# Prompt attention of a hybrid encoder step: value products with the values as weights, both heads of a pair in one output bank

## The reference

```
s = einsum('bqhc,bkc->bhqk', q_lat, ckv) + einsum('bqhr,bkr->bhqk', q_pe, kpe)
s = s.astype(jnp.float32) * MLA_SCALE
mask = (k_pos[None, :] // CHUNK) <= (q_pos[:, None] // CHUNK)      # CHUNK = 64
s = jnp.where(mask[None, None], s, jnp.finfo(jnp.float32).min)
p = jax.nn.softmax(s, axis=-1).astype(ckv.dtype)
o_lat = jnp.einsum('bhqk,bkc->bqhc', p, ckv)
mla_out = jnp.einsum('bthc,chv->bthv', o_lat, lw['w_uv']).reshape(B, T, MLA_HEADS * MLA_V)
```

## Time and profile before

| what | value |
|---|---|
| median of 3 runs | 2654.84 us (2651.89 to 2655.52) |
| profiled execution, its own time | 2655.19 us |
| its span | 2653.4 us |
| TensorE busy, share of the span | 2588.1 us, 98% |
| VectorE busy | 1689.6 us, 64% |
| ScalarE busy | 1134.7 us, 43% |
| GpSimd busy | 437.4 us, 16% |

### The profile page before, as it was taken

How to read it: one execution, slowest core, us unless ns; L and a number is a source line. 1 busy time by engine, 2 the same in 40 slices (tenths; PEclk the granted TensorE clock), 3 DMA queues, 4 the chain that set the end, 5 groups by cost and what they waited for, 6 DMA issues and landing times. The chain is left out here.

```text
span 2653.4 us, 44721 instructions
## 1 busy us (share of the span) xinstructions
PE 2588.1 (98%) x17819; PEld 2478.6 (93%) x17819; DVE 1689.6 (64%) x2725; ACT 1134.7 (43%) x1919; POOL 437.4 (16%) x366
## 2 busy tenths in 40 slices
PE   8999999999899999999999999999989999999999
PEld 8999999996679999999999999999966799999998
DVE  5666575637666776657577575764575758657473
ACT  5343344415544434334454342553164445434253
POOL 0010112102135101011210110121122341011011
PEclk9999999999999999999999999999999999999999
DMA  3322324320015132222313223234101141332231
GB/s 111 92 80 80 95 70 106 75 55 11 24 39 94 49 91 80 80 84 75 111 33 96 80 70 90 78 81 103 30 8 34 39 97 56 91 92 70 80 87 58
DMA packets 369747, 190.74 MB, mean 72 GB/s; under 512 B 38493, under 2 KB 365488, under 8 KB 369582
## 3 DMA queue, kind: packets, MB, share of 16 engines
q1 hardware_dynamic: 365582, 178.03, 24.9%
q0 software_dynamic: 4000, 10.47, 1.7%
HBM read 182.53 MB, written 5.93 MB: 71 GB/s over the span
## 5 line engine op out<-in xcount | busy, mean ns | idle before, releaser
L716 PE MATMUL ps<-xh,w 128*128 128x320 f32 x1920 | 595.1, 310 | 3.1 <-DVE css L2891 3.1
L717 PE MATMUL ps<-xl,w 128*128 128x320 f32 x1920 | 593.3, 309 | 0.0
L718 PE MATMUL ps<-xh,w 128*128 128x320 f32 x1920 | 593.3, 309 | 0.0
L1502 ACT ACTIVATE w<-raw 128x512 fp32r<-128x512 f32 (+3 forms) x372 | 316.0, 861 | 486.9 <-PE ps L718 466.1
L716 PE MATMUL ps<-hh,w 128*128 128x320 f32 x1408 | 438.0, 311 | 3.3 <-DVE ub L2295 1.2
L718 PE MATMUL ps<-hh,w 128*128 128x320 f32 x1408 | 435.1, 309 | 0.0
L717 PE MATMUL ps<-hl,w 128*128 128x320 f32 x1408 | 435.0, 309 | 0.0
L2988 POOL TENSOR_TENSOR hl<-ub,hh 128x640 fp32r<-128x640 f32 x88 | 174.5, 1983 | 1448.1 <-ACT hh L1502 1385.3
L716 PEld LDWEIGHTS ps<-xh,w 128*128 128x128 f32 x1920 | 360.4, 188 | 5.3 <-DVE css L2891 3.6
L717 PEld LDWEIGHTS ps<-xl,w 128*128 128x128 f32 x1920 | 360.4, 188 | 0.3
L718 PEld LDWEIGHTS ps<-xh,w 128*128 128x128 f32 x1920 | 360.4, 188 | 0.0
(11 more groups left out here) (408 smaller groups left out, 4663.6 us busy)
## 6 DMA issues: line engine op xcount, KB each, us to landing
raw<-in_w_ffn_in_dram SPq DMA_DIRECT2D x176, 512.0 KB
raw<-in_w_ffn_out_dram SPq DMA_DIRECT2D x192, 192.0 KB
raw<-in_w_in_dram SPq DMA_DIRECT2D x38, 512.0 KB
raw<-in_w_ffn_out_dram SPq DMA_DIRECT2D x64, 128.0 KB
wraw<-in_w_out_dram SPq DMA_DIRECT2D x8, 512.0 KB
raw<-in_w_out_dram SPq DMA_DIRECT2D x8, 512.0 KB
out_dram<-xio SPq DMA_DIRECT2D x5, 512.0 KB
xin<-in_x_prompt_dram SPq DMA_DIRECT2D x1, 2048.0 KB, 8.2
```

Of the source, the lines that this page charges most:

```text
L716: pe.matmul(out, wh, xh, start=first, stop=False, skip_group_check=loose)
L717: pe.matmul(out, wh, xl, start=False, stop=False, skip_group_check=loose)
L718: return pe.matmul(out, wl, xh, start=False, stop=last, skip_group_check=loose)
L1502: return nc.scalar.activation(out, in_, func, **kw)
```

## The change

- The value product is turned. The values (64 columns of one head, all 128 keys of a block) are the weights, and the transposed probabilities are the moving operand. The result has value columns on the partitions and 128 queries along the free dimension. The two heads of a pair go to rows 0 to 63 and 64 to 127 of bank 6, alternately. It is done for both heads at the steps of the odd head; an even head has no value product of its own.
- The even head's transposed probabilities must last until then. They go to `PTA`, ten blocks of 128 in the second half of the tile `at`; the odd head uses `ptb` as before (`weights_of`).
- The division moves. The exponents' row sums go to a new tile `sums`. Per pair VectorE takes the reciprocals (`inverse_sums`), TensorE multiplies each of them, broadcast to 64 weight columns, with the identity (`pair_rows`: 8 matmuls of 128 columns to bank 7), ScalarE copies that to `y`, and VectorE multiplies bank 6 by it into `y` (`pair_output`). The transposes of the pair's output are gone.
- TensorE's values of a pair wait for the product of the pair before (`o_sb`). The waits of values, maxima and `head_latents` on `normalise` and on the old pair output are gone, and ScalarE's copies and exponents have other ones.
- The streams' rotated latent queries go to the end of bank 1 and no longer to bank 2; `head_queries` of the second half waits for their copy.
- The first zeroing of `at` covers its first half only. The second half is zeroed after the last values, ahead of `pnew`.
- Two dummy products after the loop, not three. The last `pair_rows` stands ahead of them. The wait for the last pair's output moves ahead of the first `level_step`.
- VectorE's wait for two stores at n = 18 moves to ScalarE's copy for pair 2.

```
+    SUMS = tile(s_w, "sums", [P, 2, PT_, 2])
+    RS = tile(s_w, "rs", [P, PT_, 2])
+    AT_HALF = TILES * 2
+    ATB = AT[:, :, :, :, :].rearrange("p t e g q -> p (t e g) q")
+    PTA = ATB[:, AT_HALF:2 * AT_HALF, :]
+    def weights_of(h, i):
+        return PTB[:, i % 2, :] if h % 2 else PTA[:, i * (i + 1) // 2:(i + 1) * (i + 2) // 2, :].rearrange("p k q -> p (k q)")
...
@@ TensorE
             if h:
                 pe.wait_ge(*q_ready.nth(l, 2 * (h - 1) + half))
                 pe.wait_ge(*qk_sb.nth(l, 2 * (h - 1) + half))
+                if half:
+                    pe.wait_ge(*ql_sb.nth(l, h - 1))
...
-            if h % 2 and h > 2:
-                pe.wait_ge(*o_sb.nth(l, h // 2 - 1))
...
         def attend_values(l, n):
             h, i = divmod(n, PT_)
             pe.wait_ge(*pt_sb.nth(l, n))
-            if n >= 2:
-                pe.wait_ge(*on_sb.nth(l, n - 2))
+            if i == 0 and h > 1:
+                pe.wait_ge(*o_sb.nth(l, h // 2 - 1))
             for k in range(i + 1):
-                mm = pe.matmul(PS[:, 6 + n % 2, 0:P], PTB[:, n % 2, k * P:(k + 1) * P],
-                               VM[:, k, h // 2 * P:(h // 2 + 1) * P], start=k == 0, stop=k == i)
+                for e in range(2):
+                    mm = pe.matmul(PS[64 * e:64 * e + 64, 6, i * P:(i + 1) * P],
+                                   VM[:, k, (h - 1 + e) * 64:(h + e) * 64], weights_of(h - 1 + e, i)[:, k * P:(k + 1) * P],
+                                   start=k == 0, stop=k == i, skip_group_check=True)
             mm.then_inc(pv_ps.sem, 1)
-        def pair_output(l, pair):
-            pe.wait_ge(*on_sb.nth(l, 8 * pair + 7))
-            pe.wait_ge(*ql_sb.nth(l, min(2 * pair + 2, H - 1)))
-            for t in range(PT_):
-                mm = pe.transpose(PS[:, 2, t * P:(t + 1) * P], Y[:, pair, t * P:(t + 1) * P], IDENT[:, :])
-            mm.then_inc(ot_ps.sem, 1)
+        def pair_rows(l, pair):
+            pe.wait_ge(*rs_sb.nth(l, pair))
+            if pair:
+                pe.wait_ge(*o_sb.nth(l, pair - 1))
+            for i in range(PT_):
+                for e in range(2):
+                    mm = pe.matmul(PS[64 * e:64 * e + 64, 7, i * P:(i + 1) * P], RS[:, i, e:e + 1].broadcast_to([P, 64]),
+                                   IDENT[:, :], start=True, stop=True)
+            mm.then_inc(rb_ps.sem, 1)
...
                 if n % 8 == 2 and n > 8:
-                    pair_output(l, n // 8 - 1)
+                    pair_rows(l, n // 8 - 1)
...
-                attend_values(l, n)
+                if h % 2:
+                    attend_values(l, n)
+            pair_rows(l, H // 2 - 1)
             pe.wait_ge(*exp_sb.nth(l, NT - 1))
             held(pe)
-            spin(PS[:, 4, :], 3)
-            pair_output(l, H // 2 - 1)
+            spin(PS[:, 4, :], 2)
...
             stream_scores(l, 0)
+            pe.wait_ge(*o_sb.nth(l, H // 2 - 1))
             level_step(l, 0)
...
@@ ScalarE
+                if i == 0 and h > 3 and h % 2 == 0:
+                    act.wait_ge(*rs_sb.nth(l, h // 2 - 2))
                 run(PB[:, n % 2, 0:(i + 1) * P], PS[:, 3 + n % 2, 0:(i + 1) * P], ACT.Exp,
-                    bias=MX[:, n % 4, 1:2], accum_out=MX[:, n % 4, 2:3]).then_inc(exp_sb.sem, 1)
+                    bias=MX[:, n % 4, 1:2], accum_out=SUMS[:, h // 2 % 2, i, h % 2:h % 2 + 1]).then_inc(exp_sb.sem, 1)
...
-                if n >= 2:
-                    act.wait_ge(*pv_ps.nth(l, n - 2))
-                run(PTB[:, n % 2, 0:(i + 1) * P], PS[:, 5, 0:(i + 1) * P], ACT.Copy).then_inc(pt_sb.sem, 1)
-            def pair_output(pair):
-                act.wait_ge(*ot_ps.nth(l, pair))
-                run(Y[:, pair, 0:TP], PS[:, 2, :], ACT.Copy).then_inc(o_sb.sem, 1)
+                before = PT_ * (h // 2) + i - (2 if h % 2 and i >= 2 else 2 if h % 2 else PT_)
+                if before >= 0:
+                    act.wait_ge(*pv_ps.nth(l, before))
+                run(weights_of(h, i)[:, 0:(i + 1) * P], PS[:, 5, 0:(i + 1) * P], ACT.Copy).then_inc(pt_sb.sem, 1)
+            def pair_rows(pair):
+                act.wait_ge(*rb_ps.nth(l, pair))
+                if pair == 2:
+                    act.wait_ge(cn_stored, 32 * (l + 1))
+                run(Y[:, pair, 0:TP], PS[:, 7, :], ACT.Copy).then_inc(rb_sb.sem, 1)
...
@@ VectorE
-            def normalise(n):
-                h, i = divmod(n, PT_)
-                dve.wait_ge(*pv_ps.nth(l, n))
-                chain.link(V.reciprocal(MX[:, n % 4, 3:4], MX[:, n % 4, 2:3]))
-                at = i * P + 64 * (h % 2)
-                out = PS[:, 6 + n % 2, 64 * (h % 2):64 * (h % 2) + 64]
-                V.tensor_scalar(Y[:, h // 2, at:at + 64], out, MX[:, n % 4, 3:4], None, ALU.mult).then_inc(on_sb.sem, 1)
+            def inverse_sums(pair):
+                dve.wait_ge(*exp_sb.nth(l, 8 * pair + 7))
+                V.reciprocal(RS[:, :, :], SUMS[:, pair % 2, :, :]).then_inc(rs_sb.sem, 1)
+            def pair_output(pair):
+                dve.wait_ge(*pv_ps.nth(l, PT_ * pair + PT_ - 1))
+                dve.wait_ge(*rb_sb.nth(l, pair))
+                V.tensor_tensor(Y[:, pair, 0:TP], PS[:, 6, :], Y[:, pair, 0:TP], ALU.mult).then_inc(o_sb.sem, 1)
...
-                if n >= 3:
-                    normalise(n - 3)
+                if n % 8 == 1 and n > 8:
+                    inverse_sums(n // 8 - 1)
+                if n % 8 == 4 and n > 8:
+                    pair_output(n // 8 - 1)
...
@@ GpSimd
-            G.memset(AT[:, :, :, :, :], 0.0).then_inc(ml_zero.sem, 1)
+            G.memset(ATB[:, 0:AT_HALF, :], 0.0).then_inc(ml_zero.sem, 1)
...
-            pool.wait_ge(*pv_ps.nth(l, NT - 1))
+            pool.wait_ge(*pv_ps.nth(l, NT // 2 - 1))
             pool.wait_ge(*pn_zero.nth(l, 1))
             held(pool)
+            G.memset(ATB[:, AT_HALF:2 * AT_HALF, :], 0.0).then_inc(ml_zero.sem, 1)
             G.memset(PNEW[:, :, :], 0.0).then_inc(pn_zero.sem, 1)
```

More of the change, by code:

```diff
@@ L433, in encoder @@
     t_ps, pt_sb = event("t_ps", NT), event("pt_sb", NT)
-    pv_ps, on_sb = event("pv_ps", NT), event("on_sb", NT)
-    ot_ps, o_sb = event("ot_ps", H // 2), event("o_sb", H // 2)
+    pv_ps = event("pv_ps", NT // 2)
+    rs_sb, rb_ps, rb_sb, o_sb = (event(n, H // 2) for n in ("rs_sb", "rb_ps", "rb_sb", "o_sb"))
     cache_in = [sem(f"cache_in{c}") for c in range(CBUF)]
@@ L445, in encoder @@
     ext_zero, cs_zero = event("ext_zero", 1), event("cs_zero", 2)
-    ml_zero = event("ml_zero", 2)
+    ml_zero = event("ml_zero", 3)
     cnt_sb = event("cnt_sb", 1)
@@ L1099, in head_latents @@
                 pe.wait_ge(*ql_sb.nth(l, h - 1))
-            if h % 2 and h > 2:
-                pe.wait_ge(*o_sb.nth(l, h // 2 - 1))
             pe.matmul(PS[:, 2, 0:P], WUKT[:, h, :], QT[0:NOPE, h % 2, TP:T], start=True, stop=True)
-            pe.matmul(PS[0:ROPE, 2, P:2 * P], PAIR, QT[NOPE:P, h % 2, TP:T], start=True, stop=True)\
+            pe.matmul(PS[0:ROPE, 1, HALF:HALF + P], PAIR, QT[NOPE:P, h % 2, TP:T], start=True, stop=True)\
                 .then_inc(ql_ps.sem, 1)
@@ L1149, in gate_columns @@
             pe.wait_ge(ml_in, (l + 1) * 64)
+            pe.wait_ge(*ql_sb.nth(l, H - 1))
             pe.wait_ge(*q_ready.nth(l, 2 * H - 1))
@@ L1247, in mla @@
             level_step(l, 1)
-            pe.wait_ge(*o_sb.nth(l, H // 2 - 1))
             stream_transpose(l, 0)
@@ L1854, in latent_queries @@
                 run(QLAT[:, :, h, :], PS[:, 2, 0:P].rearrange("p (b t) -> p b t", t=TS), ACT.Copy)
-                run(QPE[0:ROPE, :, h, :], PS[0:ROPE, 2, P:2 * P].rearrange("p (b t) -> p b t", t=TS), ACT.Copy)\
+                run(QPE[0:ROPE, :, h, :], PS[0:ROPE, 1, HALF:HALF + P].rearrange("p (b t) -> p b t", t=TS), ACT.Copy)\
                     .then_inc(ql_sb.sem, 1)
             def probabilities(n):
-                i = n % PT_
+                h, i = divmod(n, PT_)
                 act.wait_ge(*nm_sb.nth(l, n))
@@ L1937, in mla @@
                 if n % 8 == 2 and n > 8:
-                    pair_output(n // 8 - 1)
+                    pair_rows(n // 8 - 1)
                 if n + 2 < NT:
@@ L1982, in mla @@
             run(KN[:, :], KPER[NOPE:QK, TP:T], ACT.Copy).then_inc(kn_sb.sem, 1)
-            pair_output(H // 2 - 1)
+            pair_rows(H // 2 - 1)
             stream_exp(0)
@@ L2615, in level @@
                     dve.wait_ge(level_in, (l + 1) * 64)
-                    dve.wait_ge(*ml_zero.nth(l, 1))
+                    dve.wait_ge(*ml_zero.nth(l, 2))
                 else:
@@ L2721, in mla @@
                     tap_of(n // 4 - 3, (0, 1, 2, 3)[n % 4])
-                if n == 18:
-                    dve.wait_ge(cn_stored, 32 * (l + 1))
                 if n % PT_ == PT_ - 1 and n // PT_ + 1 < H:
@@ L2733, in mla @@
                     V.memset(KPT[64:P, :, 0:PAST], 0.0)
-            for n in range(NT - 3, NT):
-                normalise(n)
+            inverse_sums(H // 2 - 1)
+            pair_output(H // 2 - 1)
             def stream_maximum(b):
```

4 lines of the change are left out of this document (1 added, 3 removed).

## The result

The changed kernel takes 2666.29 us (median of 5 runs, 2664.01 to 2667.03) against 2655.46 us of the kernel before beside it (5 runs): ratio 1.0046, 95% interval 1.0034 to 1.0057. It is slower by 0.46%. The forecast was 2656, with a range of 2647 to 2663.

What follows compares the result with a forecast made beforehand. No engine is full; a chain across TensorE, ScalarE and VectorE sets the length. (0.3 at the walk's end + 0.5 for clock falls) x 2 layers = 1.6 us on 2655.19, 2656.8, less 0.35 to the median: 2656, range 2647 to 2663.

Steps and rivals of the forecast that it cites:

- the half microsecond a layer for falls of the clock: TensorE's clock: one fall a layer after idle stretches costs some 1.4 us, later waits take back half, 0.5 us net.
- the walk: Step-by-step retiming (n = 4 x head + row block; T(n) its transposes): end 0.3 us later a layer.
- rival 2: Clock falls at all four idle stretches a layer: three more at 1 us net, two layers, +6, 2662; chance 0.10.
- T(30): Transposes of step 30: two VectorE memsets before its maximum leave them 0.6 us early.
- Step 13: VectorE's pair product ahead of the maximum of step 13: a gain of 0.8 us becomes a loss of 0.4.
- Step 16: VectorE's convolution piece beside GpSimd's subtractions: L1102 stays at 667.13, nothing won or lost; after it 1.4 us saved.
- Steps 18 to 21: Gate exponents on ScalarE, pair product and convolution piece ahead of a maximum: T(21) is 0.6 us early.
- T(27), T(29): Transposes of steps 27 and 29: 0.9 and 1.2 us early.
- The tail: TensorE's own work from the transposes of step 30 to the streams' first scores (L1180): +0.9 us.
- Rival 1: The halves do not overlap, 0.112 us a record: some 4 us a layer more, 2664; chance 0.08.
- Rival 4: Drain at each mode change, 0.3 us more at 7 of 20 groups: 2.1 us a layer, 2660; chance 0.06.
- Rival 3: Relief of VectorE and TensorE reaches the end: -2.5 to -4 us a layer, 2649 down to 2647; chance 0.20.

Runs made afterwards that it cites:

- with the wait filled: Changed kernel with seven dummy products in TensorE's idle stretch before the pair keys of step 4: 2664.15 us, ratio 1.0037.
- changed, no falls: Changed kernel with spare matmuls in the four stretches a layer where TensorE waits longest, product left where the change has it: 2660.98 us, ratio 1.0023.
- order, three fillings: Changed kernel with pair product one block later, memsets at block 31, spare matmuls at blocks 4, 15 and 18: 2650.03 us, ratio 0.9986.
- the run with both edits: Changed kernel with seven dummy products before the keys of block 4 and VectorE's pair product one block later: 2658.67 us, ratio 1.0018.
- that with two fillings: Changed kernel with pair product one block later, memsets at block 31, spare matmuls at blocks 4 and 18 only: 2652.79 us, ratio 0.9993.
- the run with the halves apart: Changed kernel with the loop over the two halves outside that over key blocks, in values and sums: 2673.08 us, ratio 1.0071.

## Why the prediction was wrong

The forecast, slower by 1.6 us, failed by a factor of seven, in two steps: the half microsecond a layer for falls of the clock, and the lengths of the steps in the walk.

The 14.1 us that the two stages grew split by the lengths at full clock: 2 x (90.9 - 86.9) = 8.0 us of path, and 8.4 - 2.3 = 6.1 us of more falls, in the profiled executions. The forecast had 1.6 us in all: 2 x 0.3 at the end of the walk, which already held 1.4 us a layer won from the fall at 667, hence 3.4 of path, and 2 x (0.5 - 1.4) = -1.8 of clock. Path was missed by 4.6, clock by 7.9.

**The clock: the step that failed most.** "I count one such fall a layer at 0.5 us net", after having seen the four idle stretches come. They came with nearly the forecast lengths (2.29 before the first keys, as said, 1.82, 2.09, 1.68), and rival 2, given 0.10, is nearer to what happened: not at all four waits, but once in the first layer and three times in the second, for 3 and 5.5 us. Its +6 was about the size. Two errors sit in the 0.5. One fall is not 1.4 us: the one at 636.46, 5.35 us at half clock, made T(5) and T(6) longer by 3.0 (5.14 + 4.84 against 4.23 + 2.72 with the wait filled). And "later waits take back half" did not hold there: TensorE has no idle time from 636.46 to 647.6, T(13) is 2.9 us later than without falls, and so is the end. Nor is a fall tied to its place: when one wait was filled, falls came behind others.

**The walk.** Where the transposes start, as a difference to the first layer of the kernel before, us:

```
                     T(13)  T(17)  T(21)  T(27)  T(29)  T(30)   end
forecast              +0.4   -1.4   -0.6   -0.9   -1.2   -0.6   +0.3
changed, layer 1      +3.8   +2.7   +3.8   +4.1   +3.9   +4.6   +5.4
changed, no falls     +0.9   -0.2   +0.9   +1.3   +1.1   +1.7   +2.5
order, three fillings -0.5   -1.7   -1.8   -1.4   -1.9   -2.6   -1.9
```

(third row: the first layer of the run with all four waits filled; fourth: that with three.)

- Step 13: "the gain of 0.8 is a loss of 0.4" priced the product rightly, a swing of 1.2 us, and T(13) fell by 1.35 when the product went one block later. The head start was 0.2 to 0.35 us, not 0.8.
- Step 16: "L1102 stays at 667.13: nothing won or lost" is wrong. Without falls T(16) is 1.0 us late in the changed kernel and 0.5 early with the product later: the wait ahead of it is not pinned but follows the path. The fall behind it was saved nearly as forecast, 1.2 us on T(17) against 1.4.
- Steps 18 to 21: "T(21) is 0.6 us early" is wrong. The same chain as at step 13 (copy, product, maximum) cost 1.2 us again, by the same run. I had named the product there and taken 0.8 us for it, the gate exponents and the convolution piece together.
- T(27), T(29): the "1.2 early" never came. In the stretches that TensorE paces, a values group of an odd head costs 0.33 us more than before whatever its size, and eight steps (6, 9, 14, 15, 17, 22, 23, 25) are longer by that, 2.6 us. This is a mis-sized term of the sum: 0.064 us a record and 0.1 for entering gave 0.13 to 0.22 more a group, 1.4 us on these eight. Of the 9 us taken from the even heads only part came back: without falls eleven steps (2, 3, 7, 10, 11, 16, 18, 24, 26, 27, 29) are shorter than in the kernel before, by 3.0 us together; the rest lies in TensorE's waits.
- T(30): the two memsets were seen. T(29) and T(30) together are 4.18 us before and 4.52 in the changed kernel. With the product moved they are 4.52 still, with product and memsets moved 2.85: here the memsets bind. The product moved with the memsets in place gave nothing; the memsets moved alone were not tried.
- The tail: +0.9 forecast from T(30) on, measured +0.78 (T(31) to the end 4.85 against 4.11). Right.

**Durations.** 0.064 us a record with the leaving inside: right for the groups of 16 (1.03 us), too little for the smaller ones (0.37, 0.59 and 0.80 us for 4, 8 and 12 records, from 0.09 to 0.067 us each). Rival 1 is refuted by the pairs of records 0.01 apart. Rival 4 holds in part: entering the shape costs 0.09 us, the group itself is 0.14 longer than full width would be, and the group behind it 0.1. That is 0.11 to 0.20 us a group more than the forecast took, not 0.3, and it is paid on the eight steps above, which the rival did not name. By the Trainium skill ("TensorEngine Tiling (Array Packing)", Key Properties) a change of mode drains the engine; the trace agrees that both changes cost time, and no run here shows a drain by itself. Rival 3 did not come: the best order with the clock held up is 0.4 us a layer ahead of the kernel before, not 2.5 to 4, and the moved memsets are in that.

GpSimd, the latents' bank, ScalarE's new waits: nothing of them on the path, as forecast.

What stays open: which history of TensorE makes a wait of given length bring the clock down; the 2.8 us that the rest of the span is shorter; how much the kernel before would win from the moved memsets. The split into path and falls is that of single profiled executions, and other executions of the same kernel fall elsewhere.

## What to carry to other kernels

When an edit takes work from an engine that waits anyway, compute where its idle stretches end up before counting the gain: behind a longer idle stretch TensorE may come back at half clock, and one such fall cost 3 us here, as much as all the spared matmuls of a layer gave back. An operation that has become rarer but larger is priced by what stands behind it in its engine's queue: here three products a layer stood ahead of row maxima, and moving them by one block won about three quarters of the loss. A change of shape inside a stream of matmuls has a price by the group and not by the record: 0.33 us here, which small groups don't earn back. In a chain over three engines only the late engine's work at each step counts: work removed where it isn't late buys little, and work made longer where it is late is paid in full.

## What the runs showed that I had not expected

- Less work, slower: six matmuls fewer a layer in the kernel before cost 0.19% (1.0009 to 1.0029).
- The length of a wait does not decide alone. Falls came behind 2.29 us in both layers of every run that had that wait, but also behind 1.1 us (both layers of the run with both edits, one layer of that with two fillings) and 1.30 us (the run with all four filled); 2.07 and 2.09 us were survived in one layer and not in the other.
- Matmuls into different column halves don't start in the order of the program: in the run with the halves apart the odd half's first record starts at 647.88 while three of the even half's eight, issued ahead of it, start at 647.98 and later, and the group lasts 1.51 us where 16 x 0.107 would be 1.71. The Trainium skill ("TensorE: Matmul & The Clock Gate", Packing small matmuls) has matmuls start and end strictly in order, with only weight loads pulled ahead; by the starts in this trace that does not hold across the two halves, and the measurement decides here. Ends are modelled and say nothing on it.
